# Hybrid GLA and Fourier layer: tokens arrive transposed, modulation as columns, the whole gate row late, one shared rank product

## What is computed

```python
ada = jax.nn.silu(cond) @ w_ada + b_ada            # cond: c (latents) or c_ctx (context)
shift, scale, gate = jnp.split(ada, 3, axis=-1)    # 1024 channels each
h = _rmsnorm(x, norm_g) * (1 + scale[:, None]) + shift[:, None]
z = h @ w_in                                       # q, k, v, gates, r_f, r_b, u, mg: 48 tiles of 128
g_f = log_sigmoid(r_f @ w_af + b_af) / GATE_NORM   # rank 16, and the same backward
```

## Time and profile before

| | us |
|---|---|
| median of 3 runs | 1965.89 |
| lowest, highest | 1965.18, 1968.84 |
| the profiled execution | 1968.57 |
| its span in the trace | 1966.8 |

### The profile page before, as it was taken

The page is one execution under the profiler, slowest core; times in us unless marked ns, Lnnn a source line. Parts: engine busy times, 40 slices in busy tenths (PEclk is TensorE's granted clock), DMA queues, the critical chain, the costliest instruction groups (busy, mean ns, idle before and its releaser), DMA issues.

```text
span 1966.8 us, 30215 instructions
## 1 busy us (share of the span) xinstructions
PE 1926.9 (98%) x10589; PEld 1775.1 (90%) x10589; DVE 1010.6 (51%) x1873; ACT 886.7 (45%) x1908; POOL 574.2 (29%) x646
## 2 busy tenths in 40 slices
PE   7999999999999999999999998999999999999998
PEld 2899999999999999999999996888888888898886
DVE  3878877684444433544444525666665322333333
ACT  3555667853455455444455225777732011112222
POOL 0236644143333412344333000002830033331122
PEclk9999999999999999999999999999999999999999
DMA  8577878877788778777888868656438666564433
GB/s 325 196 273 274 288 277 320 306 257 243 258 277 276 254 289 280 240 231 265 270 277 280 310 225 324 241 210 252 172 135 270 220 219 211 193 218 149 142 128 128
DMA packets 167327, 476.90 MB, mean 242 GB/s; under 512 B 14546, under 2 KB 53900, under 8 KB 158608
## 3 DMA queue, kind: packets, MB, share of 16 engines
q1 hardware_dynamic: 153360, 424.70, 63.2%
q10 hardware_dynamic: 13824, 50.34, 6.4%
HBM read 310.34 MB, written 155.20 MB: 237 GB/s over the span
## 4 chain that ended last, share of the span: by engine, by line
PE 78%; DMA 3%; POOL 2%; DVE 1%; ACT 1%; issue 1%; SPq 0%; DVEq 0%; ACTq 0%
PE bank L2116 39%; PE bank L2418 10%; PE bank L2370 10%; PE bank L2383 5%; PE bank L2247 3%; PE bank L2214 3%; PE bank L2225 2%; PE bank L2312 2%; PE bank L2236 1%; DMA x_st<-in_x 1%; POOL h_lo L997 1%; DMA qd<-qk_dec 1%; PE bank L2255 1%; PE bank L2297 1%; DMA v_ld<-v_dram 1%; PE bank L2141 1%
## 5 line engine op out<-in xcount | busy, mean ns | idle before, releaser
L2116 PE MATMUL bank<-h_hi,w_op 128*128 128x384 f32 x4032 | 1052.6, 336 | 6.0 <-DVE u L1619 3.0
L2116 PEld LDWEIGHTS bank<-h_hi,w_op 128*128 128x128 f32 x4032 | 729.9, 188 | 9.6 <-issue 9.6
L2116 PE MATMUL bank<-h_lo,w_op 128*128 128x384 f32 x2016 | 673.6, 334 | 0.0
L2116 PEld LDWEIGHTS bank<-h_lo,w_op 128*128 128x128 f32 x2016 | 378.7, 188 | 0.0
L1564 DVE TENSOR_TENSOR w_op<-w_raw,w_op 128x512 fp32r<-128x512 f32 x240 | 185.9, 776 | 110.3 <-ACT w_op L1172 106.7
L1172 ACT ACTIVATE w_op<-w_raw 128x512 fp32r<-128x512 f32 x240 | 150.2, 627 | 164.2 <-PE bank L2116 157.1
L1022 POOL TENSOR_TENSOR decs<-decs,qk_s 128x192 f32<-128x192 f32 x192 | 121.8, 671 | 334.8 <-ACT decs L1246 334.5
L2418 PE MATMUL bank<-in_a,pwa 128*128 128x512 f32 (+1 forms) x960 | 197.3, 368 | 0.0
L2418 PEld LDWEIGHTS bank<-in_a,pwa 128*128 128x128 f32 x960 | 167.3, 189 | 30.0
L2370 PE MATMUL bank<-ow,me_hi 128*128 128x512 f32 x576 | 177.4, 389 | 0.0
L1619 DVE TENSOR_TENSOR outs<-bank,u 128x384 f32<-128x384 f32 x180 | 99.6, 553 | 109.6 <-PE bank L2116 108.4
(11 more groups left out here) (240 smaller groups left out, 2655.4 us busy)
## 6 DMA issues: line engine op xcount, KB each, us to landing
w_op<-wt_dram SPq DMA_DIRECT2D x192, 512.0 KB, 5.5
wt_dram<-w_op ACTq DMA_DIRECT2D x96, 512.0 KB, 4.7
w_raw<-in_w_in SPq DMA_DIRECT2D x48, 768.0 KB, 5.9
w_raw<-in_w_in SPq DMA_DIRECT2D x24, 1024.0 KB, 6.8
qk_dec<-decs SPq DMA_DIRECT2D x48, 384.0 KB, 6.8
mg_dram<-outs SPq DMA_DIRECT2D x24, 768.0 KB, 6.9
swap<-qk_s SPq DMA_DIRECT2D x48, 192.0 KB, 5.8
v_dram<-outs SPq DMA_DIRECT2D x24, 384.0 KB, 4.9
```

The costliest lines, as they stand in the source:

```text
L2116: ins = pe.matmul(bnk, w_op[slot][:, part, k, :], h[:, j, k, :], start=(first and k == 0 and part == 0 and h is h_hi), stop=(k == HK - 1 a ...
```

## The change

- The tokens are laid out transposed in memory (`xt`), in halves of a pass, and go straight into `h32`, 1.5 MB a half. All transposes of tokens are gone. ScalarE squares them in place order into `sq`, GpSimd (VectorE at the start) folds eight channel tiles to one, and TensorE sums over the channels with a matrix of ones, one fp32 product of 384 columns for each half. ScalarE takes Ln and Exp of it, VectorE scales, and ScalarE and VectorE modulate one half each.
- The modulation is computed as columns: w_ada's blocks (128x128) are the stationary operand, the two conditioning vectors the moving one, 2 columns. There are 16 such column tiles of 8 k-steps.
- The whole gate row is made late in the last pass, with two loads of 2 MB, 32 VectorE steps and two picking products.
- The rank part (0,0), used by both blocks, is computed once: 32 matmuls a pass. ScalarE copies it and VectorE adds it for block 1.
- The loads at the start go in the order tokens, modulation block, tokens, three modulation blocks, w_raw. The first windows' weight sums move to GpSimd.
- In passes 0 and 1 both token halves are loaded at the end of window 18; squares are in windows 19 and 20, the square sums behind products 3 of window 20 and 2 of window 21, the sums of inputs in window 22.

```diff
-X_WINDOW = 18
-ADA_WINDOW = 21
+X_LOAD = 18
+X_SQUARED = ((19, 4), (20, 4))
+X_SUMMED = ((20, 3), (21, 2))
+X_SCALED = (((20, 6), (21, 0), (21, 1), (21, 2)), ((21, 4), (21, 5), (21, 6), (22, 0)))
+X_MODULATED = (((21, 3), (21, 4), (21, 5), (21, 6)), ((22, 1), (22, 1), (22, 2), (22, 2)))
+SUM_WINDOW = 22
+GATE_LOAD = 18
+ADA_WINDOW = 22
...
+            load_tokens(0, 0)
+            load_modulation(0)
+            load_tokens(0, 1)
+            load_modulation(1)
+            load_modulation(2)
+            load_modulation(3, 0, 2)
+            load_modulation(3, 2, 4)
             load_raw(0)
             load_raw(1)
...
-                        sp.dma_start(gate_dram[:, 512:D], gate_row[:, :]).then_inc(s_grst, 16)
+                        sp.dma_start(gate_dram[:, :], gate_row[:, :]).then_inc(s_grst, 16)
+                    load_summed(n + 1, 6)
+                    if p + 1 < NP and w == X_LOAD:
+                        sp.wait_ge(s_mul, 16 * (p + 1))
+                        for d in range(2):
+                            sp.wait_ge(s_qst[d], 32 * HEADS * (p + 1))
+                        for e in range(2):
+                            load_tokens(p + 1, x_half(e))
+                    if p + 1 == NP and w == ADA_WINDOW + 1:
+                        sp.wait_ge(s_grst, 16)
                         sp.dma_start(kk[0][:, 1, :], qk_dec[4, :, 1]).then_inc(s_kl[0], 16)
                         sp.dma_start(w4[:, :, :], io["w_four"]).then_inc(s_u, 16)
                         sp.dma_start(chan[:, :, :], io["chan"]).then_inc(s_u, 16)
...
+            fold_squares(0)
+            modulation(0)
+            for q in range(4):
+                scale_tokens(0, 0, q)
+            for q in range(2):
+                modulate(0, 0, q)
+            fold_squares(1)
+            low_weights(0, 0)
+            low_input(0, 0)
+            for q in range(4):
+                scale_tokens(0, 1, q)
+            for q in range(2):
+                modulate(0, 1, q)
+            modulation(1)
+            for q in (2, 3):
+                modulate(0, 1, q)
+            dve.wait_ge(s_hv, 6)
+            dve.tensor_tensor(s1[:, :, :], h32[:, 1, 0:HK, :], h32[:, 1, HK:KT, :], ALU.add).then_inc(s_s, 1)
             dve.wait_ge(s_s, 1)
             dve.tensor_tensor(s2[:, :, :], s1[:, :, :], h32[:, 0, 0:HK, :], ALU.subtract).then_inc(s_s, 1)
-            low_input(0, 0)
+            for j in range(1, 4):
+                low_weights(0, j)
             low_input(0, 1)
...
+            def columns(c, a, z):
+                j, half = c % 2, c // 2
+                for t in range(a, z):
+                    at = 2 * (KT * j + HK * half + t)
+                    for k in range(KT):
+                        ins = pe.matmul(bank[6 + half][:, at:at + 2], wmod[c][:, t, k, :], silc[:, :, k], start=k == 0, stop=k == KT - 1)
                 return ins
...
+            def square_sum(out, i):
+                pe.wait_ge(s_fold, 3 * i + 3)
+                return pe.matmul(out[:, 0:BW], ones, sq[:, 0, :], start=True, stop=True)
+
+            pe.wait_ge(s_big[0], 16)
+            columns(0, 0, 4)
+            square_sum(bank[4], 0).then_inc(s_ms, 1)
+            pe.wait_ge(s_big[1], 16)
+            columns(1, 0, 4).then_inc(s_ada, 1)
+            pe.wait_ge(s_ms, 2)
+            square_sum(bank[5], 1).then_inc(s_ms, 1)
+            pe.wait_ge(s_big[2], 16)
+            columns(2, 0, 4)
+            pe.wait_ge(s_big[3], 16)
+            columns(3, 0, 2)
+            pe.wait_ge(s_end3, 16)
+            columns(3, 2, 4).then_inc(s_ada, 1)
...
+                    if arg == 1:
...
+                        ranks(bank[use_bank[other]], ((0, 0),), True).then_inc(s_rsum, 1)
+                        ins = ranks(out, ((3, 0), (6, 1)), True)
+                    else:
+                        pe.wait_ge(s_rsum, 3 * p + 2)
+                        ins = ranks(out, ((4, 1),), False)
```

## The result

Six runs of each kernel, side by side: 1967.60 us before, 2007.61 us after (2005.52 to 2010.25), ratio 1.0205, 95% interval 1.0192 to 1.0218. The change costs 40 us. The forecast was 1994, slower, range 1979 to 2007. The sign was right, and so was the mechanism of the largest term, the start. The step on the tokens of passes 1 and 2 was wrong: it had no entry for TensorE waiting for GpSimd's fold of the squares. The time lies just above the range.

The account below looks back on a forecast made before the run. TensorE, busy 98% of the span, was taken as the bound. Terms 35.6 - 4.2 - 8.0 + 0.8 + 1.8 + 2 = +28.0 us on the 1965.89 median gave 1994, range 1979 to 2007 (8 in 10).

Parts of the forecast that it names:

- the largest term, the start: Kernel start through the first window: last modulation ready late, seventh product ending at 113.2 instead of 77.6, +35.6 us.
- the tokens of passes 1 and 2: Passes 0 and 1: transposes leave, square sums come, -8.0 us; stalls go, -2.2, VectorE lags, 3, net +0.8.
- The columns at the low clock: Start: 256 column instructions at 0.213 us, 54.6 us for four blocks; last modulation ready at 81.2; chance 0.82.
- The rival built on it: Start: columns run at full pace, 0.107 us each, costing 27 us instead of 55; time 1967; chance 0.11.
- From the modulation to the rank product: First window: VectorE's queue, stretched by GpSimd, takes 32 us instead of 30.8, bounds 26 and 36.
- Rank product, gate row: Rank product: 32 matmuls a pass instead of 40, -4.2 us; gate row: one more pair of selecting products, +1.8.
- the shared sum: Rank product: its second part waits for ScalarE's copy; 0 us, at worst 1 a pass.
- the net 0.8: Passes 0 and 1: VectorE's lag of 3 us less 2.2 of old stalls that go, +0.8 us.
- The 3 us for VectorE: Pass 0: VectorE late after waiting for w_raw and beside GpSimd's folds and sums; 3 us, bounds 0 and 8.
- End of the projection: After the passes: kk, w_four and chan load later, behind the gate row's store; +2 us, bounds 0 and 5.
- beyond the range: Rival: VectorE's lag in pass 0 repeats in every window from 19 to 22, over 2007; chance 0.02.

Follow-up runs that it names:

- e1_wide: The changed kernel with 512-column bfloat16 dummy products added on TensorE before and between the modulation columns and ahead of the second square sum; 2012.04 us.
- e3_order: The changed kernel with the start's loads in the order modulation block 0, tokens 0, block 1, tokens 1; 2004.69 us.
- e8_raw: The changed kernel with the next pass's token loads behind window 21's raw weights on SP's queue instead of ahead of them; 2005.11 us.
- e9_flat: The changed kernel without the fold of the squares: fp32r squares, each square sum eight one-pass products of 384 columns; 1993.33 us.
- b1_best: The changed kernel with row modulation, 17 dummies, no fold, reordered start loads, early first-window weights and GpSimd sums, tokens behind raw weights; 1963.25 us, ratio 0.9975 to before.
- e6_rows: The changed kernel with modulation computed as rows again and VectorE's fold ahead of the first modulation; 1977.67 us.
- b2_order: b1_best with only weights 1 and 2 split before the last modulation, and VectorE's later scalings and modulations respaced; 1961.65 us, ratio 0.9970 to before.

## Why the prediction was short

Its sum was 28.0, the profile has 39.4. By pieces, forecast against measured: to the first rank product +35.6 and +39.8, stages 0 and 1 -10.0 and -0.1, stage 2 +0.4 and +0.6, the rest +2 and -0.9. The one large miss is in stages 0 and 1. Step by step:

- **The columns at the low clock**: right in every number. 0.213 us an instruction forecast and measured, 15.4 and 15.20 for the start of block 0, 8.6 and 9.16 for the fold's wait, first product 81.2 and 81.66. It came from the earlier trace rows, and e1_wide shows that the pace follows the clock. The Trainium skill, page TensorE: Matmul & The Clock Gate, section LDWEIGHTS (loading the stationary operand), gives a load's time by its columns alone; e1_wide's 1.84 and 3.41 us for the same 16 instructions disagree with that. The rival built on it gave 1967, and is refuted.
- **From the modulation to the rank product**: 32 forecast, 35.7 measured, +3.7. The mechanism was named, its size was not: the step put the overlap at "roughly 9 us" and 5.7 us of stretch. GpSimd in fact worked beside VectorE for 14.3 us, since its own instructions are stretched too (2.66 for one that takes 1.26 by itself at 36.93), and the stretch was 7.6. That is 1.9 of the 3.7. Another 1.3 goes with the clock, which fell again in this window: from 108 to 115 us it is at 0.55 in the mean, and e3_order and e8_raw, where the last product ran at the high clock, have 34.4 instead of 35.7. The last half microsecond is open.
- **Rank product, gate row**: right. Stage 2 has these two alone: -1.4 + 1.8 = +0.4 forecast, +0.62 measured; no wait on the shared sum shows.
- **Tokens of passes 1 and 2** (made in passes 0 and 1): this is the step that failed. With its share of the rank product it said -10.0 for stages 0 and 1, and it is -0.1 (+4.45 and -4.55). It looked for what is late next on VectorE only, counted slot by slot, and took 3 us. It wrote both folds down (7 us each) as something that stretches VectorE, and put TensorE's wait for them at nothing, without a reason. The squares of the second half end near 427.0, the fold needs 7.8 us to 434.8, and the sum's place came at 431.6. The places of the three steps stood in the diff and GpSimd's rate in the earlier trace rows; when ScalarE would be done with the squares was not counted. In the trace the 9.9 us that are missing are: 6.1 of waiting for the fold, 1.7 of low clock behind the first wait, which before does not have there (1.00 from 410 to 450 us), and 2.0 of other waits beyond the net 0.8 that the step had. e9_flat, without the fold, prices it at 6.4 and 2.9 us together with its stretching of VectorE. The 3 us for VectorE were of about the right size: 1.3, 1.9 and two waits under 1 us on its additions.
- **End of the projection**: +2 forecast. The channel product waits 0.77 us as before, the late v load 3.95 instead of 2.66; over the rest that is -0.9, in a piece that scatters by 6. Nothing of the 2 can be claimed.
- **The bounds.** 1979 to 2007 left out 2007.6 by 0.6 us. The lower one does not follow from the bounds of the terms: with 26, 0 and 0 they give 1983. The upper one, said to be 2007 and a little over, is 2009 with 36, 8, 5 and 1 a pass for the shared sum. The upper bound held for each term but the tokens; it had no entry for a chain over three engines (squares, fold, sum) being longer than the slots it is given. That the time came so near the range is in part luck, since the rest of the program was 2.9 us under its forecast. The rival "beyond the range" named VectorE's lag, which was the smaller part.

What stays open: how the fold's cost divides into the wait and the stretching of VectorE, whether the late w_raw costs anything (e8_raw says 2 us, b1_best nothing), and what of VectorE's last 2.2 us in pass 0 is its own queue and what GpSimd's sums in window 22. That GpSimd's work be made shorter there was not tried.

## What to carry to other kernels

Ask of a small product which operand streams. Here TensorE, with two moving columns, had its weight loads busy for 26.7 of 27 us and the clock did not come up; 256 such instructions cost 55 us where 64 with 512 moving columns cost 31 (e6_rows), or 28 where the clock was up from the first (b1_best). When work is moved onto an idle engine, ask both who it slows and who waits for its result; a chain across three engines needs its whole length between its slots, not the busy time of one. And where TensorE is the bound, a late start is not made up: here 9.2 us taken out of the first 55 came back as 9 to 10 at the end.

## What the runs showed of the hardware

- **The clock came up behind dummy products and fell again under the columns.** In e1_wide the stretch from 57 to 59 us is at 1.00 behind 36 wide products; with two more wide products at 59.01 and columns again from 59.44 it is back at 0.50 by 61. b1_best has 17 wide dummies ahead of the first row, in time that TensorE had idle, and its first block of rows ran at full pace: 7.03 us, where e6_rows' first eight instructions alone took 6.45.
- **VectorE and GpSimd slow each other.** A 1536-element subtraction takes 1.76 us by itself and 2.83 beside GpSimd's 512-element sums, which take 1.26 by themselves and 2.66 so. Instructions with one tensor input are hit as well: four scale-and-shift steps (TENSOR_SCALAR) that take 1.65 us took 3.65 in b2_order beside GpSimd's sums. The Trainium skill, page SBUF — State Buffer, section Who interferes with whom, says that the one cause of contention is a pair of ports that the two engines share under an exclusive lock, and that a VectorE instruction with two inputs in SBUF contends with a GpSimd instruction that reads SBUF. The numbers of the two-input subtraction agree with it: one instruction of each by itself makes 1.76 + 1.26 = 3.0 us, against the 2.8 and 2.7 us that they take side by side.
- **Two pieces of code that were not touched** differ by up to 1.6 us (stage 1) and 6 us (the rest) between kernels. The first goes with the clock behind the second square sum: e3_order (370.2) has a mean of 0.68 from 808 to 812 us, after (368.7) 1.00 from 805 to 815, both behind the same wait of 2.69 us. For the second no cause was looked for.
